# Six modulation rows of a two-block transformer kernel: summed over partitions by two terms in the rounded format instead of one full float32 product

## What is computed

```python
c_act = jax.nn.silu(c)
for layer in range(DEPTH):
    mod = c_act @ ada_w[layer] + ada_b[layer]
    sh1, sc1, g1, sh2, sc2, g2 = jnp.split(mod, 6, axis=-1)
    h = modulate(rmsnorm(x, norm_mix[layer]), sh1, sc1)
    ...
    x = x + g1[:, None, :] * y
    h = modulate(rmsnorm(x, norm_ffn[layer]), sh2, sc2)
    x = x + g2[:, None, :] * peer_ffn(h, ...)
```

## Time and profile before

| what | value |
|---|---|
| median of the runs | 2224.89 us |
| span of the profiled execution, first to last instruction | 2222.0 us |
| TensorE matmul busy | 1963.9 us, 88% |
| VectorE busy | 1560.3 us, 70% |
| ScalarE busy | 1033.6 us, 47% |
| GpSimd busy | 628.7 us, 28% |
| DMA | 761.24 MB, 343 GB/s on average |

### The profile page before, as it was taken

The page is one execution under the profiler, slowest core; times in us unless marked ns, Lnnn a source line. Parts: engine busy times, 40 slices in busy tenths (PEclk is TensorE's granted clock), DMA queues, the critical chain, the costliest instruction groups (busy, mean ns, idle before and its releaser), DMA issues. The chain is left out here.

```text
span 2222.0 us, 24054 instructions
## 1 busy us (share of the span) xinstructions
PE 1963.9 (88%) x8090; PEld 1240.2 (56%) x8090; DVE 1560.3 (70%) x2943; ACT 1033.6 (47%) x2177; POOL 628.7 (28%) x552
## 2 busy tenths in 40 slices
PE   5999989987777888899999988888898889999998
PEld 5987845432222333479885544343343326888987
DVE  6987877676667775678878876676777755565554
ACT  4345545544444444444445644444455434544443
POOL 1000255544444444000014444444344430200000
PEclk9999999999999999999999999999999999999999
DMA  8897799999999999786589999999999995343553
GB/s 332 296 378 261 312 421 421 420 421 422 421 421 421 421 422 421 291 338 226 206 301 421 414 421 420 421 421 421 421 411 421 421 421 191 115 145 132 189 189 133
DMA packets 112396, 761.24 MB, mean 343 GB/s; under 512 B 12832, under 2 KB 13600, under 8 KB 26128
## 3 DMA queue, kind: packets, MB, share of 16 engines
q0 software_dynamic: 76480, 548.94, 59.7%
q1 hardware_dynamic: 34832, 207.74, 25.2%
q10 hardware_dynamic: 960, 3.01, 0.4%
HBM read 758.60 MB, written 1.05 MB: 342 GB/s over the span
## 5 line engine op out<-in xcount | busy, mean ns | idle before, releaser
L1046 PE MATMUL pair<-uv,p_diag 128*128 128x512 f32 x1352 | 653.2, 619 | 114.3 <-ACT p_diag L2374 112.4
L1743 DVE CUSTOM_DVE_ANT_0 uv<-uv,p_h 128x1024 f32<-128x1024 f32 x338 | 413.7, 1224 | 242.6 <-DMA uv<-in_peer_uv,p_idx 240.7
L573 POOL DMA_INDIRECT uv<-in_peer_uv,p_idx x338 | 398.3, 1179 | 522.8 <-PE pair L1046 385.9
L1046 PEld LDWEIGHTS pair<-uv,p_diag 128*128 128x128 f32 x1352 | 243.8, 193 | 493.5 <-ACT p_diag L2374 271.4
L1314 DVE TENSOR_TENSOR ring_low<-ring,ring_high 128x2048 fp32r<-128x2048 f32 x143 | 326.5, 2297 | 102.6 <-ACT ring_high L2156 101.4
L2366 ACT ACTIVATE p_act<-p_dot 128x1 f32<-128x1 f32 x512 | 103.5, 202 | 627.6 <-DVE p_dot L1743 625.5
L2156 ACT ACTIVATE ring_high<-ring 128x2048 fp32r<-128x2048 f32 x144 | 272.2, 1908 | 187.8 <-DMA ring<-in_ret_w_in 64.5
L725 PE MATMUL pair<-hT_high,ring_high 128*128 128x256 f32 x960 | 287.3, 299 | 0.2
L1046 PE MATMUL pair<-uv_high,p_diag 128*128 128x512 f32 x464 | 229.2, 625 | 52.5 <-ACT p_diag L2374 52.5
L725 PE MATMUL pair<-hT_low,ring_high 128*128 128x256 f32 x960 | 272.1, 283 | 0.0
L725 PE MATMUL pair<-hT_high,ring_low 128*128 128x256 f32 x896 | 254.1, 284 | 0.0
(11 more groups left out here) (413 smaller groups left out, 2660.1 us busy)
## 6 DMA issues: line engine op xcount, KB each, us to landing
ada<-in_ada_w SPq DMA_DIRECT2D x50, 512.0 KB, 5.9
ring<-in_ret_w_in SPq DMA_DIRECT2D x24, 1024.0 KB, 8.2
ring<-in_sgu_w_in SPq DMA_DIRECT2D x24, 1024.0 KB, 6.6
ring<-in_w_up SPq DMA_DIRECT2D x16, 1024.0 KB, 4.8
ring<-in_w_down SPq DMA_DIRECT2D x16, 1024.0 KB, 4.8
mod<-in_ada_w SPq DMA_DIRECT2D x30, 512.0 KB, 5.7
ring<-in_peer_w_query SPq DMA_DIRECT2D x12, 1024.0 KB, 8.5
ring<-in_sgu_w_out SPq DMA_DIRECT2D x12, 1024.0 KB, 4.9
```

Of the source, the lines that this page charges most:

```text
L573: nc.gpsimd.indirect_dma_start(uv_rows[SLOT[l][s]].rearrange("p a d -> p (a d)"), None, experts, bass.IndirectOffsetOnAxis(ap=p_idx[:, k:k ...
L1046: mm = nc.tensor.matmul(acc[:, half, :], p_diag[:, n % DIAGS, :], v[:, half * 512:(half + 1) * 512], start=(k == 0), stop=(k == PICKS - 1))
L1743: V.tensor_tensor_reduce(out=u, in0=u, in1=p_h[:, s // PICKS, :], scale=1.0, scalar=0.0, op0=ALU.mult, op1=ALU.add, accum_out=p_dot[:, n % ...
```

## The change

Rows 4, 5, 6, 8, 9 and 10 are no longer multiplied by the ones in float32. GpSimd copies the row into the rounded format (`row_high`, in the memory of the gather slot `spare`), subtracts it from the row, and writes the rest over the row itself (`row_low`). TensorE then makes two products per half, ones by high and ones by low, both in the rounded format. The ones are kept in that format; for the other uses they are read as float32 as before.

```diff
+IN_TERMS = (4, 5, 6, 8, 9, 10)
...
+        row_high = nc.alloc_sbuf_tensor_at("row_high", [P, 2, D], F32R, offset=spare_base)
+        row_low = nc.alloc_sbuf_tensor_at("row_low", [P, 2, 3, D], F32R, offset=mod_base)
...
+            def split_row(v):
+
+                n = IN_TERMS.index(v)
+                high, low = terms_of(v)
+                pool.wait_ge(ada_used, (v - 1) * KD)
+                if n >= 2:
+                    pool.wait_ge(small_ready, SMALL[("mod", IN_TERMS[n - 2], 1)] + 1)
+                nc.gpsimd.tensor_copy(high, summed(v)).then_inc(row_raised, 1)
+                pool.wait_ge(row_raised, n + 1)
+                nc.gpsimd.tensor_tensor(low, summed(v), high.bitcast(F32), ALU.subtract).then_inc(row_split, 1)
+
             lows(low_by_pool[0:1])
             pool.wait_ge(bias_zero, 1)
-            modulation_rows(range(2, 8))
+            modulation_rows(range(2, 6))
+            for v in (4, 5):
+                split_row(v)
+                modulation_rows((v + 2,))
+            split_row(6)
+            pool.wait_ge(small_ready, SMALL[("mod", 6, 1)] + 1)
             gathers(0)
...
-            modulation_rows(range(9, 12))
+            modulation_rows(range(9, 10))
+            pool.wait_ge(uv_used, TT * PICKS)
+            for v in (8, 9):
+                split_row(v)
+                modulation_rows((v + 2,))
+            split_row(10)
+            pool.wait_ge(small_ready, SMALL[("mod", 10, 1)] + 1)
...
             def sum_mod(v):
 
+                if v in IN_TERMS:
+                    pe.wait_ge(row_split, IN_TERMS.index(v) + 1)
+                    for half in range(2):
+                        name, columns = ("mod", v, half), slice(half * 512, (half + 1) * 512)
+                        open_small(name)
+                        high, low = terms_of(v)
+                        nc.tensor.matmul(small_of(name)[:, :], exact_ones[:], high[:, columns], start=True, stop=False)
+                        nc.tensor.matmul(small_of(name)[:, :], exact_ones[:], low[:, columns], start=False, stop=True).then_inc(small_ready, 1)
+                    return
                 pe.wait_ge(ada_used, (v - 1) * KD)
```

More of the change, by code:

```diff
@@ L254, in two_blocks @@
         ring_high = sb("ring_high", [P, RH, BK, BN], F32R)
+        spare_base = (nc.sbuf_base + 31) // 32 * 32
         spare = sb("spare", [P, 2, D])
+        row_high = nc.alloc_sbuf_tensor_at("row_high", [P, 2, D], F32R, offset=spare_base)
+        row_low = nc.alloc_sbuf_tensor_at("row_low", [P, 2, 3, D], F32R, offset=mod_base)
         x = sb("x", [P, TT, D])
@@ L259, in two_blocks @@
         ident = sb("ident", [P, P])
-        ones = sb("ones", [P, P])
+        exact_ones = sb("exact_ones", [P, P], F32R)
+        ones = exact_ones[:].bitcast(F32)
         junk_base = (nc.sbuf_base + 31) // 32 * 32
@@ L369, in two_blocks @@
         ada_used, bias_zero = sem("ada_used"), sem("bias_zero")
+        row_raised, row_split = sem("row_raised"), sem("row_split")
         mod_gain_in, mod_gain_used = sem("mod_gain_in"), sem("mod_gain_used")
@@ L457, in summed, with terms_of @@
             return mod[:, SUMMED[v - 2] // 3, SUMMED[v - 2] % 3, :]
+        def terms_of(v):
+            place = SUMMED[v - 2]
+            return row_high[:, IN_TERMS.index(v) % 2, :], row_low[:, place // 3, place % 3, :]
         taken_after = []
```

## The result

The changed kernel takes 2227.41 us (median of 21 runs, 2225.69 to 2233.47), the kernel before 2224.74 us (21 runs, 2221.81 to 2228.1). The ratio is 1.0019, with a 95% interval of 1.0013 to 1.0025: 4.2 us slower (2.9 to 5.6); the medians differ by 2.7. The forecast was 2228.3 us, by +3.4. Time and range held, the sum in part by luck: by the profile each of its four terms is off by 1.3 to 1.5 us, retention and row 9 too cheap, row 8 and row 10 too dear, and these errors cancel.

What follows compares the result with a forecast made beforehand. TensorE was taken to set the pace at retention's end, VectorE at the end of `sgu_u` and in the mixing. Terms -1.1 + 0 + 2.2 + 2.7 - 0.4 = +3.4 on 2224.9 gave 2228.3 us, range 2221 to 2233.

Steps and rivals of the forecast that it cites:

- TensorE's gain, 0.2 us for each of four instructions: Six row sums on TensorE: products follow after 0.23 us instead of 0.43, 0.8 us a row, 4.8 us for six.
- first rival: Splits fit VectorE's gaps or lock little: retention gives 2.4, row 10 gives 0.4, so 2222.1 us; chance 0.22.
- The copy, 1.9 us: GpSimd's copy of each row into the rounded format takes 1.90 us, like the nearest operation of the same shape.
- One engine stands while the other works: VectorE with two SBUF inputs and GpSimd reading SBUF hold shared ports in turn, each for its whole instruction.
- served in turn: Waiting for the port lock is served in turn; VectorE always going first (2239 us) was thought hardly likely.
- Row 9, +2.2 through VectorE: In SGU, TensorE stands 2.9 us for the split and VectorE's lowering starts 2.2 us later, carried into the mixing.
- third rival: TensorE's stand at row 9 also costs clock: 2230.0 to 2231.7 us; chance 0.25 together with the last rival.
- Row 10, +2.7 - 0.4: In the mixing, copy holds VectorE 1.1 us, subtraction 1.6; the shorter sum lets `scale_row` start 0.4 us earlier.
- Retention, -1.1: Three shorter sums gain 2.4 us; TensorE waits 1.3 us for the last block's low part at the end.
- row 4 is ready some 25 us, row 5 some 40 us before, 0.8 us each is gained: In retention, both rows are ready long before TensorE's sums, so each gains 0.8 us.
- Row 8, 0: In SGU, the split is done long before; TensorE gains 0.8 us and gives it back waiting for VectorE's block.

Runs made afterwards that it cites:

- e1: The changed kernel without GpSimd's splits: VectorE writes the six rows rounded, TensorE makes two rounded products, low part left out; 3.1 us under the kernel before.
- e3: The changed kernel with row 9 not split and summed in fp32 as before; 0.4 us over the kernel before (-1.6 to 2.4).
- e9: The changed kernel with the sum of row 9 put behind the next block of columns; 1.6 us over the kernel before (-0.4 to 3.6).
- e8: The changed kernel run again as it is, in another group; 2.9 us over the kernel before (0.9 to 4.9).
- e7: The changed kernel with GpSimd making the copy of each of the six rows twice; 9.3 us over the kernel before (6.5 to 12.5).
- e4: The changed kernel's GpSimd queue order and waits, but nothing split and all rows summed in fp32; 0.9 us over the kernel before (-1.1 to 2.9).
- e5: The changed kernel with only rows 4, 5 and 6 split, rows 8 to 10 in fp32; 1.1 us under the kernel before (-3.1 to 0.9).
- e11: The changed kernel with only rows 4 and 6 split; 1.3 us under the kernel before (-3.3 to 0.7).
- e2: The changed kernel's six splits on GpSimd, but TensorE sums in fp32 without waiting for them; 4.4 us over the kernel before (2.4 to 6.7).
- e6: The changed kernel with only rows 8, 9 and 10 split, rows 4 to 6 in fp32; 4.0 us over the kernel before (2.0 to 6.0).
- e12: The changed kernel with only rows 4, 8 and 9 split and row 9's sum one block later; 1.1 us under the kernel before (-3.1 to 0.9).

## Why the forecast was right, and where it was wrong

- **TensorE's gain, 0.2 us for each of four instructions**: right. L796 and L797 start at 170.67, 170.91 and 171.14. With nobody paying, 3.1 us of the 4.8 reach the end by the runs of e1 (1.1 to 5.1), near the 2.8 of the first rival; in its profiled execution it is 1.6 at `scale_row`.
- **The copy, 1.9 us**: too long. It is 1.03 alone, near the lower bound of 0.93.
- **One engine stands while the other works**: right, at each place where two SBUF inputs met. Where it was wrong is "served in turn": a copy of 1.03 us has a record of 6.36, so it waited 5.3 us, for two steps of VectorE. This and the short copy cancel, so the split of row 9 ended at 1027.2 where the forecast had 1027.9, and TensorE stood 2.5 us (forecast 2.9).
- **Row 9, +2.2 through VectorE**: the size of the loss was too small and its path wrong. VectorE's lowering, held to 3.35 us, ended at 1029.3 where before's ended at 1029.2: its wait for ScalarE ahead of it had shrunk. At the mixing it waited 4.39 us for TensorE. The loss is 3.4 to 3.5 us, of which the clock is 1.7: what the forecast had put into its third rival. e3 (the row taken out) and e9 (the stand alone taken out) show it.
- **Row 10, +2.7 - 0.4**: mis-sized. The step held by the subtraction (1.97 us instead of 0.69, the first line before, the second after) costs 1.28 where 1.6 was forecast, and the copy, forecast at 1.1, holds up next to nothing (0.07): it fell beside a step with an input in PSUM. TensorE's wait behind it is 2.33 us instead of 1.06. Through `scale_row` it is +0.93 net; 1.8 where the clock falls as well (e3, e9).

```profile
1074.19 0.69 DVE L1916 TENSOR_TENSOR s_t<-s_u,s_t 128x512 f32<-128x512 f32 x1
```
```profile
1077.04 1.97 DVE L1958 TENSOR_TENSOR s_t<-s_u,s_t 128x512 f32<-128x512 f32 x1
```

- **Retention, -1.1**: the step "row 4 is ready some 25 us, row 5 some 40 us before, 0.8 us each is gained" failed. It asked only whether the split is in time and left out what it does to VectorE, 2.7 and 2.5 us, which comes late to the statistics of the heads. TensorE's waits there are 1.6 + 0.9 us (0.2 + 0.9 in e8), and 0.4 to 0.6 at the end, where 1.3 was forecast. -2.4 + 2.5 + 0.4 = +0.5, against +0.36 measured; e8 by the same sum -0.7, measured -0.46. Five executions with all three rows stand at +0.85, +0.36, -0.11, -0.46 and -1.47 (e7, which copies twice, at +0.11), so the mean is -0.2, and the 1.5 us by which +0.36 misses the forecast is partly this spread. What moves them is not settled: VectorE's waits for DMAs in 110 to 145 us, up to the first split, are 6.0 us in the change and 4.8 before, and it comes to the first split 2.2 us late in the change and 0.7 in e8.
- **Row 8, 0**: the part from 917.5 to 986.9 is 0.5 to 1.4 us shorter in eight kernels that split row 8 and sum it in two terms, and 0.0 to 0.6 in e1, e4, e5 and e11, which do not split it; in e2, which splits it and sums in fp32, it is unchanged. TensorE gives the 0.8 us of row 8 back at once (in the change it waits 1.17 us for `ring_low` right behind that sum). What is shorter lies ahead of it: TensorE's wait for `ring_low` near 981 is 1.3 to 1.7 us in the eight and 2.0 to 2.4 in before, e1, e2, e4, e5 and e11. Behind it the clock fell in before, e1, e2 and e5 (below), but not in e4 and e11, and e11 is no shorter for it. How splitting row 8 brings this about isn't shown.

One after the other, in the change: retention and what follows it up to 917.5 us (VectorE's first step on `p_h` for SGU) +0.7, `sgu_v` up to 986.9 -1.4, row 9 +3.5, row 10 +0.9, and -0.8 behind it, of which 0.9 is the shorter DMA wait near 1140. That is +3.0 at the gathers' indices; the span is 2.6 longer. Of the 4.2 us by the runs the rest is not accounted for.

## What to carry to other kernels

Before work is put on an idle GpSimd, look at what VectorE does beside it. Where its steps have two SBUF inputs and no slack, a GpSimd instruction of these traces either held one of them up or waited for it; beside steps without two SBUF inputs (row 8) the copy took 1.04 and the subtraction 2.42 us, and nothing was held. Here the six shorter sums gave 3.1 us (e1), the splits' hold on VectorE cost 4.4 (e2), and TensorE's stand came on top. Ask of a split not only whether it is in time for its consumer, but who else waits for the engine that it holds. And when the consumer is TensorE, move its instruction behind other work rather than let it stand: a stand of 2.5 us cost 4.2 with the clock behind it. Moving it (e9) took the loss in `sgu_u` away in the profile and 1.3 to 2.6 us off the time, not all: the clock then fell behind row 10.

## What the runs showed of the hardware

- A GpSimd instruction that waits while VectorE works is not always next. In all seven traces in which row 9 is split (the change, e2, e6, e7, e8, e9, e12) the copy's record is 6.36 or 6.37 us: VectorE's step of 3.41 us and then one of 2.28 us that followed without a gap went first. At rows 4 and 5 it took 3.03 or 3.04, behind a single step of 2.29 us, and there it did go ahead of the step that followed without a gap. So neither order is the rule, and what decides is not shown. The Trainium skill tells of the exclusive hold in "SBUF — State Buffer" (section "SBUF: two separate sides"): whichever of the two starts first has the shared ports for its whole instruction. The traces agree (a step of 1.28 us takes 2.06 beside the copy of 1.03). Which engine comes next is told by these rows alone.
- Whether a stand of TensorE costs the clock is not told by its length alone. Near 981 it waited for `ring_low`. A wait of 2.21 us (before, e5) was followed by windows of 0.64 and 0.51 or 0.82 and 0.50, and so were 2.11 (e1) and 2.36 us (e2). But 2.23 us (e11) and 2.02 (e4) were followed by 1.00, as were the 1.3 to 1.7 us of the others. Near 1079 a stand of 2.33 us was followed by 1.00 in the change, e6 and e8, and by 0.50 in e9, e3 and e2. In the first three the clock had fallen once already, behind row 9; in e7 it had as well, and fell again behind 3.03 us. What decides it is not shown. Windows of before, of the change and of e11 for the first place:

```profile
982.00:984.00 2.00, 2.00 (x8) 1.57 (x7) 1.79 (x2) 0.00 (x0) 0.00 (x0) 0.64 0.90 328
```
```profile
982.00:984.00 2.00, 2.00 (x11) 1.63 (x10) 1.73 (x2) 0.66 (x1) 0.00 (x0) 1.00 0.89 313
```
```profile
982.00:984.00 2.00, 2.00 (x10) 1.62 (x9) 1.73 (x3) 0.16 (x1) 0.00 (x0) 1.00 0.81 252
```
